# Hybrid decoder step on one core: the last two output tiles by token halves, the final scale on GpSimd, key products one chunk sooner, the sample values' split moved to the head of its lists, and the root's transposes moved into the sixth chunk

## The reference

```python
def rms_norm(x, g):
    xf = x.astype(jnp.float32)
    y = xf * lax.rsqrt(jnp.mean(xf * xf, axis=-1, keepdims=True) + RMS_EPS)
    return (y * g.astype(jnp.float32)).astype(x.dtype)
...
        h = rms_norm(xp, norm_g[l])
        u, gp, q, k, v, ga = split_proj(h, w_in[l])
        pm, pbuf = pool_mix(u, zero_buf, 0, pool_w[l], pool_scale[l])
        a = dilated_attn_prompt(q, k, v, slopes)
        xp = xp + merge_out(pm, gp, a, ga, w_out[l], xp.dtype)
...
    y_prompt = rms_norm(xp, final_norm_g)
...
# sample tokens, for each of three patterns over the cache:
        s = jnp.einsum('bshe,bsnhe->bhsn', qf, kg) * scale
...
        o = jnp.einsum('bhsn,bsnhe->bshe', p, vg) / den_t[..., None]
```

## Time and profile before

| what | value |
|---|---|
| median of 3 runs | 902.86 us (902.83 to 903.67) |
| the profiled execution | 903.18 us, its span 901.3 us |
| mean granted TensorE clock | 0.989 of full |
| busy: PE, DVE, ACT, POOL | 859.9, 565.9, 402.5, 52.1 us |
| share of the span | 95%, 63%, 45%, 6% |
| DMA | 121.36 MB, mean 135 GB/s |

### The profile page before, as it was taken

One profiled execution on the slowest core, in us unless ns is written; L12 is line 12 of the kernel. 1 busy time (PEld: TensorE's weight loads), 2 busy tenths in 40 slices (PEclk: granted clock), 3 DMA queues, 4 the chain that ended last, 5 costly groups with the idle time before them and its releaser, 6 DMA issues. The chain is left out here.

```text
span 901.3 us, 17338 instructions
## 1 busy us (share of the span) xinstructions
PE 859.9 (95%) x7014; PEld 847.0 (94%) x7014; DVE 565.9 (63%) x1035; ACT 402.5 (45%) x896; POOL 52.1 (6%) x96
## 2 busy tenths in 40 slices
PE   7999999999999999999999999999989999999991
PEld 7999999999999999999999999999978999999990
DVE  5546866668676768667786767687779633333332
ACT  5745335524543453355246434533555433444333
POOL 3000000001000000100010000000000000000000
PEclk9999999999999999999999999999999999999996
DMA  8363455364526635553554266355565434434324
GB/s 300 113 166 99 122 149 146 93 161 133 142 83 149 174 91 134 140 148 93 141 158 129 86 155 174 87 131 150 150 167 155 127 107 120 124 109 124 110 59 189
DMA packets 207048, 121.36 MB, mean 135 GB/s; under 512 B 7576, under 2 KB 201760, under 8 KB 206432
## 3 DMA queue, kind: packets, MB, share of 16 engines
q1 hardware_dynamic: 202520, 111.20, 44.7%
q0 software_dynamic: 4448, 9.05, 3.1%
HBM read 108.04 MB, written 12.63 MB: 134 GB/s over the span
## 5 line engine op out<-in xcount | busy, mean ns | idle before, releaser
L547 PE MATMUL pj<-mov_hi,w_hi 128*128 128x260 f32 x2048 | 423.0, 288 | 0.5 <-DVE mov_lo L1425 0.5
L547 PE MATMUL pj<-mov_hi,w_lo 128*128 128x260 f32 x2048 | 412.0, 283 | 0.0
L547 PE MATMUL pj<-mov_lo,w_hi 128*128 128x260 f32 x2048 | 411.4, 282 | 0.0
L547 PEld LDWEIGHTS pj<-mov_hi,w_hi 128*128 128x128 f32 x2048 | 315.3, 189 | 2.1 <-DVE mov_lo L1425 0.7
L547 PEld LDWEIGHTS pj<-mov_lo,w_hi 128*128 128x128 f32 x2048 | 315.8, 188 | 0.0
L547 PEld LDWEIGHTS pj<-mov_hi,w_lo 128*128 128x128 f32 x2048 | 315.4, 188 | 0.0
L1103 DVE TENSOR_TENSOR w_lo<-w_raw,w_hi 128x640 fp32r<-128x640 f32 (+1 forms) x192 | 166.3, 866 | 213.5 <-ACT w_hi L745 212.6
L745 ACT ACTIVATE w_hi<-w_raw 128x640 fp32r<-128x640 f32 (+1 forms) x192 | 147.6, 769 | 187.2 <-PE pj L547 183.5
L801 ACT ACTIVATE pt_hi<-ps_t 128x128 fp32r<-128x128 f32 (+1 forms) x64 | 26.2, 436 | 78.9 <-PE ps_t L555 72.2
L1186 DVE TENSOR_TENSOR pt_lo<-ps_t,pt_hi 128x128 fp32r<-128x128 f32 (+1 forms) x64 | 29.6, 484 | 43.0 <-ACT pt_hi L801 43.0
L785 ACT ACTIVATE arena<-arena,stat 128x128 f32<-128x128 f32 (+1 forms) x64 | 35.5, 555 | 35.8 <-DVE stat L1172 35.8
(11 more groups left out here) (161 smaller groups left out, 710.3 us busy)
## 6 DMA issues: line engine op xcount, KB each, us to landing
w_raw<-in_w_in SPq DMA_DIRECT2D x96, 320.0 KB, 3.3
w_raw<-in_w_in SPq DMA_DIRECT2D x48, 384.0 KB, 3.6
arena<-in_cache_k_win SPq DMA_DIRECT2D x16, 384.0 KB, 5.4
arena<-in_cache_v_win SPq DMA_DIRECT2D x16, 384.0 KB, 8.1
w_raw<-in_w_out SPq DMA_DIRECT2D x16, 384.0 KB, 3.7
w_raw<-in_w_out SPq DMA_DIRECT2D x16, 320.0 KB, 3.0
arena<-row_scratch POOLq DMA_DIRECT2D x8, 512.0 KB, 5.0
arena<-in_cache_k_win SPq DMA_DIRECT2D x8, 512.0 KB, 6.4
```

What stands on the lines that cost most here:

```text
L547: mm = pe.matmul(pj[a][h][:, 0:HT], w, m[:, k, HT * h:HT * h + HT], start=(k == 0 and i == 0), stop=(c == 2 and k == KT - 1 and i == 2))
```

## The change

Five edits.

1. `kq` of `USUAL` is (17, 18, 19) and was (18, 19, 20). `FINAL` stays.
2. `av_hi` and `av_lo` move from `late` to `early` in the same step, ahead of that step's weight split.
3. The root's five transposes move from behind chunk 4 to within chunk 5, behind its k = 13.
4. Tiles 14 and 15 run by token halves: all 16 k of tile 14 for h = 0, then of tile 15 for h = 0, then both for h = 1 (`half_chunk`). The six weight chunks stay in SBUF for that: `w_at` puts tile 14's in `pt_hi`/`pt_lo` and `av_hi`/`av_lo`, and tile 15's in the three slots. The waits of `split_hi` on TensorE change accordingly. For each h the epilogue is made for two token tiles (and the 8 sample rows with h = 1): eviction, transposes (`turn_half`), residual (`half_add`), squares 256 wide on ScalarE (`half_squares`) and VectorE (`half_square`), sum, root (`half_root`), scaling by halves of 1024 columns, and stores of 512 KB.
5. The multiplication by the gain of tiles 14 and 15 is on GpSimd, behind the squares, and the scaling waits for it (`half_scaled`).

```diff
 
-USUAL = Plan(qk=(7, 12), s=(8, 13), kn=13, ur=15, kq=(18, 19, 20), ns=20, pt=22,
+USUAL = Plan(qk=(7, 12), s=(8, 13), kn=13, ur=15, kq=(17, 18, 19), ns=20, pt=22,
              vm=(23, 23, 24), va=(24, 25), av=26, mix=(19, 21), gate=20)
...
+
+        def w_at(n):
+
+            m = n - IN_CHUNKS - 3 * (KT - 2)
+            if m not in (0, 1, 2):
+                return w_hi[:, n % SLOTS], w_lo[:, n % SLOTS]
+            if m == 2:
+                return tuple(a[:, 0:CK * P].rearrange("p (k x) -> p k x", k=CK)
+                             for a in (av_hi, av_lo))
+            at = CK * P * m
+            return tuple(a.rearrange("p j x -> p (j x)")[:, at:at + CK * P].rearrange(
+                "p (k x) -> p k x", k=CK) for a in (pt_hi, pt_lo))
 
         def last_chunk(d):
...
+            for h in range(2):
+                for i, part in enumerate((slice(0, D_HALF), slice(D_HALF, D_MODEL))):
+                    sp.wait_ge(f_out, 2 * h + i + 1)
+                    sp.dma_start(yp[:, 2 * h, part], y[:, 2 * h, part]).then_inc(f_st, 16)
+                    sp.wait_ge(f_out_a, 2 * h + i + 1)
+                    sp.dma_start(yp[:, 2 * h + 1, part], y[:, 2 * h + 1, part]).then_inc(f_st, 16)
...
+                        pe.wait_ge(rs_done, 4)
+                        for i in range(QT):
+                            turn(ps_s[:, P * i:P * i + P], rstd[:, i:i + 1].to_broadcast([P, P]))
+                        turn(ps_m[:, 0:NB], rstd[0:NB, QT:QT + 1].to_broadcast([NB, P]),
+                             NB).then_inc(rs_turned, 1)
                 mm.then_inc(w_used, 1)
...
+            def half_chunk(d, c, h):
+
+                n = IN_CHUNKS + OUT_N[d, c]
+                if h == 0 and c == 0:
+                    pe.wait_ge(yt_done, d - 1)
+                pe.wait_ge(w_lo_done, n + 1)
+                lo, hi = CHUNKS[c]
+                for k in range(lo, hi):
+                    whi, wlo = (w[:, k - lo, :] for w in w_at(n))
+                    for i, (w, m) in enumerate(((whi, mov_hi), (whi, mov_lo), (wlo, mov_hi))):
+                        mm = pe.matmul(pj[d % 2][h][:, 0:HT], w, m[:, k, HT * h:HT * h + HT],
+                                       start=(k == 0 and i == 0), stop=(k == KT - 1 and i == 2))
+                if c == 2:
+                    mm.then_inc(half_done, 1)
 
...
-                chunk(step)
-                if step == 4:
-                    pe.wait_ge(rs_done, 4)
-                    for t in range(QT):
-                        turn(ps_s[:, P * t:P * t + P],
-                             rstd[:, t:t + 1].to_broadcast([P, P]))
-                    turn(ps_m[:, 0:NB], rstd[0:NB, QT:QT + 1].to_broadcast([NB, P]),
-                         NB).then_inc(rs_turned, 1)
+                if step < IN_CHUNKS + OUT_N[KT - 2, 0]:
...
-            turn_y(KT - 1)
...
+            def turn_half(d, h):
+                q = d % 2
+                rows_to, smp_to = ((ps_t, ps_m), (ps_s, ps_o))[q]
+                pe.wait_ge(half_out, 2 * h + q + 1)
+                if h == 0:
+                    pe.wait_ge(y_added, KT - 2)
+                for t in (0, 1) if h == 0 else (2, 3):
+                    tr = turn(rows_to[:, P * t:P * t + P], y_t[q][:, P * t:P * t + P])
+                if h == 1:
+                    tr = turn(smp_to[0:NB, 0:P], y_t[q][:, SEQ:NT])
+                tr.then_inc(half_turned, 1)
+
+            for h in range(2):
+                for d in (KT - 2, KT - 1):
+                    for c in range(3):
+                        half_chunk(d, c, h)
+                        if d == KT - 2 and h == 0 and c == 0:
+                            turn_y(KT - 3)
+                        if d == KT - 1 and c == 0:
+                            turn_half(KT - 2, h)
+                        if d == KT - 2 and h == 1 and c == 0:
+                            turn_half(KT - 1, 0)
+            turn_half(KT - 1, 1)
 
 
...
                 act.wait_ge(raw_in[n % SLOTS], raw_count(n))
-                if n >= 3:
+                if n >= last_chunk(KT - 1) - 2:
+                    act.wait_ge(w_used, n - 4)
+                elif 3 <= n < last_chunk(KT - 2) - 2:
                     act.wait_ge(w_used, n - 1)
-                act.activation(w_hi[:, n % SLOTS, 0:hi - lo, :], w_raw[:, n % SLOTS, 0:hi - lo, :],
+                act.activation(w_at(n)[0][:, 0:hi - lo, :], w_raw[:, n % SLOTS, 0:hi - lo, :],
                                ACT.Copy).then_inc(w_hi_done, 1)
...
+                if j == p.av:
+                    act.wait_ge(av_add, 2 * pr + 2)
+                    if pr > 0:
+                        act.wait_ge(av_sum, 2 * pr)
+                    act.activation(av_hi[:, :], kv[:, 0, :], ACT.Copy).then_inc(av_hi_done, 1)
...
-            y_out(KT - 1)
-            y_square(KT - 1)
...
+            def half_evict(d, h):
+                q = d % 2
+                act.wait_ge(half_done, 2 * h + q + 1)
+                if h == 0:
+                    act.wait_ge(y_turned, d - 1)
+                act.activation(y_t[q][:, HT * h:HT * h + HT], pj[q][h][:, 0:HT],
+                               ACT.Copy).then_inc(half_out, 1)
...
+            def half_squares(h):
+                cols = slice(P * (KT - 2), D_MODEL)
+                act.wait_ge(half_added, 2 * h + 2)
+                for i, t in enumerate((0,) if h == 0 else (2, QT)):
+                    act.wait_ge(y_sq, 5 * (KT - 2))
+                    if h + i > 0:
+                        act.wait_ge(half_sq, h + i)
+                    n = P if t < QT else NB
+                    src = y[:, t, cols] if t < QT else y_s[0:NB, cols]
+                    act.activation(sq_wide[0:n, :], src, ACT.Square,
+                                   accum_out=ss_y[0:n, t, KT - 2:KT - 1]).then_inc(half_sq, 1)
+
+            for h in range(2):
+                half_evict(KT - 2, h)
+                half_evict(KT - 1, h)
+                half_squares(h)
+                act.wait_ge(f_ms, h + 1)
+                own = slice(2, 5) if h else slice(0, 2)
+                act.activation(sd[:, own], ms[:, own], ACT.Sqrt).then_inc(f_sd, 1)
+                act.wait_ge(f_rs, 4 * h + 4)
+                act.wait_ge(half_scaled, h + 1)
+                t = 2 * h + 1
+                for part in (slice(0, D_HALF), slice(D_HALF, D_MODEL)):
+                    act.activation(y[:, t, part], y[:, t, part], ACT.Copy,
+                                   scale=rstd[:, t:t + 1]).then_inc(f_out_a, 1)
...
+            for h in range(2):
+                own = slice(2 * h, 2 * h + 2)
+                pool.wait_ge(half_sq, 1 + 2 * h)
+                pool.wait_ge(half_sq_v, h + 1)
+                for d in (KT - 2, KT - 1):
+                    gf = x_res[d % 2][:, SEQ + P:SEQ + 2 * P]
+                    cols = slice(P * d, P * d + P)
+                    ys, yss = y[:, own, cols], y_s[0:NB, cols]
+                    if h == 1:
+                        pool.tensor_tensor(yss, yss, gf[0:NB, :], ALU.mult)
+                    o = pool.tensor_tensor(ys, ys, gf.unsqueeze(1).to_broadcast([P, 2, P]), ALU.mult)
+                o.then_inc(half_scaled, 1)
+
 
         @block.vector
...
+                if j == p.av:
+                    dve.wait_ge(av_hi_done, pr + 1)
+                    dve.tensor_tensor(av_lo[:, :], kv[:, 0, :], av_hi[:, :].bitcast(F32),
+                                      ALU.subtract).then_inc(av_split, 1)
...
-                if j == p.av:
-                    dve.wait_ge(av_hi_done, pr + 1)
-                    dve.tensor_tensor(av_lo[:, :], kv[:, 0, :], av_hi[:, :].bitcast(F32),
-                                      ALU.subtract).then_inc(av_split, 1)
...
+                rows_from, smp_from = ((ps_t, ps_m), (ps_s, ps_o))[q]
+                cols = slice(P * d, P * d + P)
+                own = slice(2 * h, 2 * h + 2)
+                dve.wait_ge(half_turned, 2 * h + q + 1)
+                dve.wait_ge(xr_in[q], 48 * (d // 2) + 48)
+                o = dve.tensor_tensor(
+                    y[:, own, cols],
+                    rows_from[:, 2 * P * h:2 * P * h + 2 * P].rearrange("p (t x) -> p t x", t=2),
+                    x_res[q][:, 2 * P * h:2 * P * h + 2 * P].rearrange("p (t x) -> p t x", t=2),
+                    ALU.add)
...
+                    o = dve.tensor_tensor(y_s[0:NB, cols], smp_from[0:NB, 0:P],
+                                          x_res[q][0:NB, SEQ:SEQ + P], ALU.add)
+                o.then_inc(half_added, 1)
+
+            def half_square(h):
+                src = y[:, 2 * h + 1, P * (KT - 2):D_MODEL]
+                dve.wait_ge(half_added, 2 * h + 2)
+                dve.tensor_tensor_reduce(out=sq_wide_v, in0=src, in1=src, scale=1.0, scalar=0.0,
...
+            for h in range(2):
+                own = slice(2, 5) if h else slice(0, 2)
+                half_add(KT - 2, h)
+                half_add(KT - 1, h)
+                half_square(h)
+                dve.wait_ge(half_sq, 1 + 2 * h)
+                dve.wait_ge(half_sq_v, h + 1)
```

(9 more changed lines are left out.)

75 lines of the change are left out of this document (37 added, 38 removed).

## The result

| | median us | runs | lowest to highest |
|---|---|---|---|
| before | 903.27 | 6 | 902.83 to 904.52 |
| after | 886.63 | 6 | 885.87 to 886.99 |

The ratio is 0.9813, with an interval of 0.9801 to 0.9825. That is 16.6 us less where 14.8 was forecast. The profiled execution took 886.28 us, its span 884.4, 16.9 less than before's.

A forecast was written before the change was run, and what follows sets the result against it. TensorE, busy 859.9 of 901.3 us, was taken to bound the kernel. Terms 1.0 + 4.2 + 2.3 + 0.2 - 0.2 + 7.3 = 14.8 us less took the median from 902.86 to 888.0, range 885.8 to 892.3.

The forecast's parts named there:

- What bounds the kernel: Whole kernel: TensorE is busy 859.9 of 901.3 us, its waits are few, and 20.9 us lie behind its last matmul.
- Keys: Seven usual pairs: with the keys' product a chunk sooner, TensorE's bias waits of 0.60 each go, 4.2 us less.
- the cover of 3.7 us: Usual pairs: slack before TensorE's first product behind chunk 19, hiding the 2.44 us two key instructions add on VectorE.
- `av`: Pairs: split put ahead of the weight split; seven `av_lo` waits of 0.33 go, 2.3 us, plus 0.2 in the last pair.
- Root: Chunk 5: the 1.22 us wait goes, a new one of 0.2 for tile 0's eviction comes; 1.0 us less.
- Halves, weights and evictions: Tiles 14 and 15: weights in time, margins 1.0 and 1.3 us; eviction cover thinnest, 0.3; two more transposes cost 0.2.
- Behind the last matmul: Epilogue and stores of the second half: 20.9 us becomes 13.6, with the root ready at 4.3 and bytes deciding the end.
- So GpSimd ends last, by 0.9: Behind the last matmul: GpSimd's four gain products are ready at 5.2 us, the root at 4.3.
- slow stores: Kernel's end: smaller stores move at two thirds of the rate, adding 2.6 us; chance 0.15, shared with slow GpSimd products.
- starving: Last tiles: chunk 191's low part comes late and TensorE stands 3.8 us, giving 891.8; chance 0.12.
- renamed wait: Pairs: TensorE waits for something else instead, and 6.5 us stay, giving 894.5; chance 0.07.
- its luck: Last pair: the granted clock's fall, costing about 1.7 us, fails to come (886.3) or lasts twice as long (889.7); chance 0.04.

## Why the prediction was right, point by point

The total (forecast 14.8, measured 16.6) lies within the range, and the errors had opposite signs: the terms ahead of the last matmul were too small (keys, `av`, root), the one behind it too large. That they nearly cancel is luck.

- **What bounds the kernel**, right. Each edit alone gave time, and within the noise they added up.
- **Keys**, mechanism right, size too small. No wait is listed in the seven pairs, and none appeared at the cover of 3.7 us. The step that failed is "0.60 each": the price is 0.78. Seven times is 5.4, forecast 4.2. In the seventh pair 0.2 of it did not come. There VectorE ended the bias at 593.44 and TensorE's transposes started at 593.59, 0.19 later than the rows before them allow, too little to be listed. The kernel with the keys alone has the same 0.2 (80.37 for 80.18).
- **`av`**, the same. "7 x 0.33" should have been 7 x 0.56 or so, 3.9 instead of 2.3. In the fifth pair 0.4 was lost (79.94 and 82.59 for 79.63 and 82.51). VectorE stood 2.33 us there, until 443.60, for the load of cached values, the longest of its three such waits (3.2 us in all); `av_lo` came late, and TensorE waited for it once more:

```profile
455.24 0.47 PE L737 MATMUL ps_m<-av_hi,ones_r 128*128 128x512 f32 x1 [0.16 <-DVE av_lo L1418]
```

That belongs to the execution: the kernel in which GpSimd waits for the mean has 79.62 and 82.51 in these places. In the last pair most of the 0.9 was given back by `mov_lo`: from the last `av_hi` matmul to the end of the last one it takes 181.62 before and 182.52 now, 0.9 more, and the forecast was 0.7 + 0.2 for two transposes.
- **Root**, mechanism right, size a little too small: 1.0 forecast, 1.26 for the edit alone. Of the changed kernel, the root's transposes on TensorE, without idle time, the eviction that hangs on them, and TensorE's first rows of chunk 6, which needs its banks:

```profile
37.84 0.60 PE L592 MATMUL ps_s<-tab,stat 128*128 128x128 f32 x4
```

```profile
39.32 0.76 DVE L1231 SCALAR_TENSOR_TENSOR arena<-pj,rstd_bc 128x260 f32<-128x260 f32 x2 [1.34 <-ACT rstd_bc L1020]
```

```profile
39.82 0.40 PE L563 MATMUL pj<-mov_hi,w_lo 128*128 128x260 f32 x2
40.14 0.51 PE L563 MATMUL pj<-mov_hi,w_hi 128*128 128x260 f32 x2
40.49 0.40 PE L563 MATMUL pj<-mov_lo,w_hi 128*128 128x260 f32 x2
```

The eviction ends at 40.08, 2.24 behind the transposes' start, and TensorE could have started chunk 6 at 39.82 + 0.24 = 40.06. No idle time is listed there, and yet the new wait of 0.2 has come: from row to row it is 0.32 and 0.35 where 0.24 each is usual, 0.19 more. What the sum left out is the refill behind the old wait: 1.22 + 0.17 = 1.39, less 0.19, is 1.20, and the transposes take 0.68 where they took 0.72.

- **The head** was in no term: in the changed kernel's profile chunk 5 starts at 35.66, and before's could have started at 36.06, 0.4 later. Over the kernels shown this start lies between 35.6 and 37.2. This is luck of one execution, and it belongs to the noise of each profile, not to the change.
- Together, ahead of the last matmul: 0.4 head, 1.3 root, 1.2 in pair 0 up to its `av_hi`, 8.4 in the seven distances, less 0.9: 10.4. Forecast was 7.5, and the distances alone should have given 6.5.
- **Halves, weights and evictions**, right, the thin cover too. The changed kernel in order of time, low part of chunk 191, and the last eviction of tile 14 with the transposes that need it:

```profile
853.91 0.81 DVE L1199 TENSOR_TENSOR w_lo<-w_raw,w_hi 128x640 fp32r<-128x640 f32 x1
...
865.45 0.36 ACT L1066 ACTIVATE arena<-pj 128x260 f32<-128x260 f32 x1
...
865.94 0.38 PE L592 MATMUL ps_t<-tab,arena 128*128 128x128 f32 x2
```

The low part is ready at 854.72, and chunk 191 starts at about 856.1, a margin of 1.4 where 1.3 was forecast. The eviction ends at 865.81 and TensorE comes 0.13 later, without an idle time; the margin was forecast at 0.3.

- **Behind the last matmul**, the step that failed is "ready at 4.3" for the root. It came at 5.5, since its mean was held 1.37 us instead of 0.17 by GpSimd's products. "So GpSimd ends last, by 0.9" thus went wrong by its second half only: GpSimd's time was right (5.1, forecast 5.2; wide ones 0.71 where 0.83 was taken, narrow ones 0.45 where 0.4), but the sum had treated two engines beside each other as free. The first store was 0.4 late. The bytes then took some 0.3 longer, at 0.40 instead of 0.42 MB per us, and the end came 1.9 behind them instead of 1.8: 14.4 for 13.6.
- **The Trainium skill's figures**: GpSimd's product took 1.7 times VectorE's (0.71 to 0.41, 0.45 to 0.27), where the Trainium skill, "GPSIMD Engine Reference", section 3.1, says about twice; the trace roughly agrees. The four took 2.2 us with their overlaps, between the 1.7 estimated by the page's rate and the forecast's 2.5. The rule for big DMAs (the Trainium skill, "DMA: Bandwidth & Descriptors", section Bandwidth) did not bind here: 512 KB stores, several in flight, moved 399 to 408 GB/s, and the kernel with 1 MB stores, 397 to 422, ended 0.4 later.
- **The rivals.** None came: no slow stores, no starving, hardly a renamed wait (only `mov_lo` and one `av_lo`), and the clock fell behind the last pair's wait as before, so its luck stayed out of the result. The 1.7 us put on that fall is borne out roughly by the two profiles without it, 1.4 and 1.55 shorter in that pair.

## What to carry to other kernels

Price a wait of a pipelined engine by the distance between the starts around it, not by the idle time listed; here 0.33 and 0.60 listed were 0.56 and 0.78 real. Work put on GpSimd beside a short chain on VectorE is not hidden: look for an instruction of VectorE that takes longer beside it than alone, and first try the same products in VectorE's own list (0.6 us better here) or fused into an instruction that runs anyway (1.3 better). And size an experiment by a distance inside the kernel where the start differs by up to 1.6 us from run to run.

## What was not expected of the hardware

- A VectorE instruction on 3 columns took 1.36 to 1.37 us beside GpSimd's four products (0.17 alone), in two forms, and ended near the start of the last product. A reciprocal at the same place took 0.18. The same work beside the first half's products took less. VectorE and GpSimd in the changed kernel, some eight microseconds ahead of the last matmul's end:

```profile
861.47 1.43 POOL L1175 TENSOR_TENSOR arena<-arena 128x256 f32<-128x256 f32 x2 [188.04 <-ACT arena L1078]
861.64 0.59 DVE L1646 TENSOR_SCALAR stat<-stat 128x2 f32<-128x2 f32 x1
```

- A TensorE wait of 1.8 us was followed by a fall of the granted clock to half in some executions (the root's edit alone) and not in others (the changed kernel).
